# HGRN heads of a fused decoder step: the next head's projections placed between the parts of this head

## The chip, the cores and the metric

One core of a Trainium2 chip runs the whole program. The metric is the device time of one execution in microseconds (us).

## The reference, cut to what matters

The model is a two-layer decoder step for 512 prompt positions and 8 sample sequences of one position each. Layer 0 mixes tokens with two groups of heads side by side: 8 HGRN2 heads and Mamba heads. The change is in the HGRN2 heads alone. For one head, with a forget gate f, a query q, a value v and an output gate g, all four projected from the same normalised input h (1024 wide, 128 columns per head and projection):

```python
q_a, f_a, i_a, g_a, ... = split(h @ w_in_ab)
log_f = log(lb + (1 - lb) * sigmoid(f));  k = (1 - lb) * sigmoid(-f);  q = silu(q)
S_t = diag(f_t) S_{t-1} + k_t v_t^T       # state, 128 x 128 a head
o_t = S_t^T q_t                           # prompt in chunks, samples one step each
out = rmsnorm(o) * hg_norm * silu(g)
```

The prompt is computed in chunks: inside a chunk the attention of queries over keys with the decay between them, across chunks through the state. The samples take one step each from a stored state.

## The kernel before

All data lie feature-major: 128 features on the partitions, 520 tokens (512 prompt, 8 sample) along the free axis, held in PSUM as two banks of 260 columns. Weights arrive from HBM in a ring of two slots (`weight_ring`), one load of 1 MB holding a head's query and forget weights, the next its value and gate weights. A projection is done in three passes, for nearly full float32 precision: weights rounded to fp32r times rounded inputs ("hi"), bf16 weights times the inputs' remainder, and the weights' remainder in bf16 times bf16 inputs ("rest"). Each pass is 8 tiles x 2 halves, 16 matmuls of 260 columns. ScalarE makes the hi and bf16 copies of the weights (`hgrn_cut`, L1616 and L1617) and VectorE the remainder (`hgrn_cut`, L2381); two buffers of weight parts take turns, so a cut waits for the projection before last.

Each engine has one instruction stream in a fixed order written out by hand, with semaphores between them. For each of the 8 heads (`head(h, more)` on each engine, a hardware loop for seven and the last one apart), the order on TensorE is: VALUE projection (banks 6, 7); GATE projection (banks 4, 5), with the five transposes of the values ahead of its rest pass (L1127, they wait for ScalarE's copy of the values, L1833); the key-query products of "level 0" and level 64 (L1152); four transposes of the decayed keys (L1133); the products of the other six levels (L1152), each of which waits until VectorE has taken the one before last out of the two PSUM banks; the four state updates of the chunks (L1159); the values of the samples spread to all partitions (L1163, banks 6, 7); the FORGET projection of the next head (banks 2, 3); the prompt's outputs (L1175, L1177); the samples' outputs, eight matmuls of one column (L1181, 16 instructions in the trace); the QUERY projection of the next head (banks 0, 1) with the sum of squares (L867, `sums`) after its hi pass.

ScalarE has, per head: the cut of the GATE weights; SiLU of the query (L1823); the exponentials of the cumulated decay, of the keys' decay and of seven levels (L1826 to L1831); the copy of the values (L1833); the token-major values (L1835 to L1837); SiLU of the gate (L1839); the cuts of the next FORGET and QUERY; the copy of the transposed keys (L1847); the samples' products of key and value (`sample_products`, L1808); the next head's two sigmoids (`forget_gates`, L1801 and L1802) and the cut of VALUE; the squares of the outputs (L1855, L1856); the logarithm of the next forget gate (`forget_log`, L1814); the inverse RMS (`inv_rms`, L1572 and L1574).

VectorE has, per head: remainder of GATE (L2381); fourteen subtractions for the level decays (L2441, L2442) and fourteen multiplications by queries and keys (L2453, L2454); remainders of the next FORGET and QUERY; the three bf16 parts of the sample values (L2462 to L2467); the eight levels taken out of PSUM (L2482, L2475, L2485), L2488; the update of the eight sample states (L2494, eight operations; `s_new`); the states of the chunks (L2499, L2502; `h_s`); `forget` of the next head (L2422, L2423, remainder of VALUE, and L2426, the scan that cumulates the logarithm); the normalised output (L2509, L2510, L2513; `h_done`).

GpSimd loads and stores the states by DMA, SyncE loads the weights.

## Time and profile before

| | us |
|---|---|
| median of 3 runs (lowest, highest) | 3025.14 (3020.88, 3027.26) |
| the profiled execution, its time | 3025.36 |
| its span in the profile | 3023.8 |
| TensorE matmuls busy | 2807.6 (93%) |
| VectorE busy | 1406.4 (47%) |
| ScalarE busy | 1355.1 (45%) |
| mean granted TensorE clock | 0.969 of 2.4 GHz |

The HGRN heads lie from 499 us to 839 us of the span. How to read the rows below: a time ahead of a line is the start of the first instruction of a merged run, the next number is how long the run took, `xN` how many instructions it holds, and the bracket at the end is the idle time of that engine before it and what ended it. A run that begins before the one ahead of it has ended is pipelined. PEclk is the granted TensorE clock: 1.00 is 2.4 GHz, 0.50 is 1.2 GHz.

### The profile page before, as it was taken

The page shows a single profiled execution, that of the slowest core. Times are in us where ns is not written, and L with a number is a line of the kernel's source. Part 1 is how long each engine was busy: PE and PEld are TensorE (multiplying, and loading weights), DVE is VectorE, ACT ScalarE, POOL GpSimd, SP SyncE. Part 2 cuts the span into 40 slices and gives each one's busy share as a digit, 9 for nine tenths or more (in the row PEclk, how much of TensorE's full clock was granted, in tenths as well). Part 3 has the DMA queues.
Part 4 walks back from the last instruction along what each step waited for, and adds up shares of the span by engine and source line. Part 5 has one row for each costly group of instructions (what it writes and reads, how often), then busy time and mean ns, then how long its engine had stood idle before and what let it go on. Part 6 is the DMA issues. An engine that isn't in the chain of part 4 may idle for free.

```text
span 3023.8 us, 60783 instructions
## 1 busy us (share of the span) xinstructions
PE 2807.6 (93%) x24504; PEld 2354.1 (78%) x24504; DVE 1406.4 (47%) x2893; ACT 1355.1 (45%) x2099; POOL 45.1 (1%) x78
## 2 busy tenths in 40 slices
PE   6999997887888989999999999999989989999997
PEld 3899885777667868799888899888856557789996
DVE  2444327666657763634425444333433434544433
ACT  3444337666643444634345434344423334544443
POOL 0000000000000000000000000000000000000000
PEclk8999998989999989999999999999999999999998
DMA  6223442121212224222343123432365435322221
GB/s 241 84 97 123 161 148 86 71 85 64 78 68 89 88 94 184 89 83 95 138 177 117 70 97 123 166 143 79 128 187 161 148 112 191 123 74 94 102 96 67
DMA packets 58281, 349.35 MB, mean 116 GB/s; under 512 B 7537, under 2 KB 7874, under 8 KB 28578
## 3 DMA queue, kind: packets, MB, share of 16 engines
q1 hardware_dynamic: 52274, 322.85, 30.0%
q0 software_dynamic: 5872, 24.59, 2.3%
q8 instruction: 98, 1.61, 0.2%
q14 instruction: 37, 0.30, 0.0%
HBM read 334.96 MB, written 12.45 MB: 115 GB/s over the span
## 4 chain that ended last, share of the span: by engine, by line
PE 76%; DVE 8%; ACT 8%; issue 3%; DVEq 2%; DMA 2%; ACTq 0%; PEldq 0%; SPq 0%; POOL 0%; PEld 0%
PE PS L940 54%; PE PS L918 2%; PE PS L954 2%; PE PS L867 2%; PE PS L1436 1%; PE PS L978 1%; PE PS L1418 1%; PE PS L1421 1%; PE PS L874 1%; PE PS L1397 1%; ACT hgrn_w_hi L1616 1%; DMA weight_ring<-in_mla_pairs 1%; PE PS L899 1%; ACT sub_out L1831 1%; PE PS L962 1%
## 5 line engine op out<-in xcount | busy, mean ns | idle before, releaser
L2167 DVE TENSOR_TENSOR w_rest<-weight_ring,w_hi 128x1024 bf16<-128x1024 f32 (+1 forms) x268 | 320.8, 1197 | 857.4 <-ACT w_hi L1616 857.2
L1616 ACT ACTIVATE w_hi<-weight_ring 128x1024 fp32r<-128x1024 f32 (+1 forms) x284 | 294.8, 1038 | 889.1 <-PE PS L940 886.0
L940 PE MATMUL PS<-hid_hi,w_hi 128*128 128x260 f32 x2432 | 326.9, 286 | 0.0
L940 PEld LDWEIGHTS PS<-hid_hi,w_hi 128*128 128x128 f32 x2432 | 299.2, 188 | 2.3
L940 PE MATMUL PS<-hid_rest,w_bf 128*128 128x260 bf16 x2432 | 298.4, 274 | 0.0
L940 PE MATMUL PS<-hid_bf,w_rest 128*128 128x260 bf16 x2432 | 296.7, 274 | 0.0
L1617 ACT ACTIVATE w_bf<-weight_ring 128x1024 bf16<-128x1024 f32 (+1 forms) x284 | 289.7, 1020 | 0.0
L940 PEld LDWEIGHTS PS<-hid_bf,w_rest 128*128 128x128 bf16 x2432 | 235.6, 97 | 36.5
L940 PEld LDWEIGHTS PS<-hid_rest,w_bf 128*128 128x128 bf16 x2432 | 223.9, 97 | 38.6
L940 PE MATMUL PS<-gu_hi,w_hi 128*128 128x260 f32 x1232 | 168.7, 288 | 0.0
L940 PEld LDWEIGHTS PS<-gu_hi,w_hi 128*128 128x128 f32 x1232 | 152.8, 188 | 14.1 <-issue 11.2
L940 PE MATMUL PS<-gu_rest,w_bf 128*128 128x260 bf16 x1232 | 152.3, 274 | 0.0
L940 PE MATMUL PS<-gu_bf,w_rest 128*128 128x260 bf16 x1232 | 151.3, 273 | 0.0
L940 PEld LDWEIGHTS PS<-gu_bf,w_rest 128*128 128x128 bf16 x1232 | 119.1, 97 | 18.6
L940 PE MATMUL PS<-hgrn_in_rest,hgrn_w_bf 128*128 128x260 bf16 x1056 | 133.0, 276 | 0.0
L940 PE MATMUL PS<-hgrn_in_bf,hgrn_w_rest 128*128 128x260 bf16 x1056 | 130.7, 274 | 0.0
L940 PE MATMUL PS<-mixer_in_hi,hgrn_w_hi 128*128 128x260 f32 x864 | 122.7, 297 | 6.3 <-ACT hgrn_w_hi L1616 5.1
L940 PEld LDWEIGHTS PS<-gu_rest,w_bf 128*128 128x128 bf16 x1232 | 112.8, 97 | 19.7
L940 PEld LDWEIGHTS PS<-mixer_in_hi,hgrn_w_hi 128*128 128x128 f32 x864 | 112.3, 198 | 9.7 <-ACT hgrn_w_hi L1616 5.4
L940 PEld LDWEIGHTS PS<-hgrn_in_bf,hgrn_w_rest 128*128 128x128 bf16 x1056 | 102.3, 97 | 16.2
L940 PEld LDWEIGHTS PS<-hgrn_in_rest,hgrn_w_bf 128*128 128x128 bf16 x1056 | 97.5, 98 | 18.7
L874 PE MATMUL PS<-consts 128*128 128x512 bf16 x337 | 86.6, 414 | 2.9 <-DVEq L558 2.9
(487 smaller groups left out, 4471.8 us busy)
## 6 DMA issues: line engine op xcount, KB each, us to landing
weight_ring<-in_ffn_gu SPq DMA_DIRECT2D x88, 1024.0 KB, 4.8
ada_chunks<-in_ada_w SPq DMA_DIRECT2D x40, 1536.0 KB, 6.6
weight_ring<-in_ffn_wd SPq DMA_DIRECT2D x32, 1408.0 KB, 6.0
weight_ring<-in_w_hgrn SPq DMA_DIRECT2D x16, 1024.0 KB, 4.8
weight_ring<-in_ada_w SPq DMA_DIRECT2D x8, 1536.0 KB, 7.2
weight_ring<-in_w_ssm SPq DMA_DIRECT2D x8, 1536.0 KB, 6.9
weight_ring<-in_mla_pairs SPq DMA_DIRECT2D x8, 1536.0 KB, 6.5
weight_ring<-in_w_out_ab SPq DMA_DIRECT2D x8, 1024.0 KB, 7.9
```

What stands on the lines that cost most here:

```text
L867: last = pe.matmul(PS[0:rows, bank + hf, 0:HT], weights[k], moving[k][:, hf * HT:(hf + 1) * HT], start=(k == 0), stop=(k == n - 1))
L874: pe.matmul(PS[:, bank, :], STEADY[:, 0:P], STEADY[:, 0:4 * P], start=True, stop=True)
L899: last = pe.matmul(PS[:, bank, 0:HT], w[:, k * P:(k + 1) * P], x[:, k, side(hf)], start=start and w is w_hi, stop=stop and w is w_rest)
L918: last = pe.matmul(PS[:, bank, 0:HT], w[:, k * P:(k + 1) * P], x[:, first + k, side(hf)], start=start and w is w_hi and k == 0, stop=stop ...
L940: last = pe.matmul(PS[:, bank + hf, 0:HT], w[:, k * P:(k + 1) * P], x[:, first + k, hf * HT:(hf + 1) * HT], start=start and w is w_hi and ...
L954: last = pe.matmul(PS[q * QR_:(q + 1) * QR_, 4, 0:3 * P], CS[:, k, :], weights[:, k * 3 * P:(k + 1) * 3 * P], start=(k < 4), stop=(k >= 4))
L962: last = pe.matmul(PS[:, 5, c * NSEQ:(c + 1) * NSEQ], MS[:, c * P:(c + 1) * P], const("fold")[:, 0:NSEQ], start=True, stop=True)
L978: last = pe.matmul(PS[:, 7, 0:HT], ONES, Y[:, c, side(hf)], start=(c == 0), stop=(c == DC - 1))
L1397: last = pe.matmul(PS[:, 4, :], WF[:, first:first + P], CKV[:, k, 0:NP_], start=(k == 0), stop=(k == RC - 1))
L1616: act.activation(hi, src, ACT.Copy).then_inc(w_hi_ready, 1)
L1617: act.activation(bf, src, ACT.Copy).then_inc(w_bf_ready, 1)
L2167: tt(WL_[:, buf, 0:n], W[:, slot, j * DC * P:j * DC * P + n], WH[:, buf, 0:n].bitcast(F32), ALU.subtract).then_inc(w_rest_ready, 1)
```

## The change

On TensorE a head now runs: all eight levels without a break; the transposes of the keys; FORGET of the next head (banks 2, 3); the state updates; the spread of the sample values; QUERY of the next head; the outputs of prompt and samples; VALUE of the next head (now banks 2, 3), with the sum of squares behind its hi pass; GATE of the next head, with the next head's value transposes ahead of its rest pass (now in banks 2, 3). The first head's VALUE and GATE stand ahead of the loop. In the last head 12 and 24 filler matmuls stand where FORGET and QUERY would be, instead of 30.

On ScalarE the cut of the next FORGET moves ahead of the token-major value copies, the next sigmoids and the cut of VALUE ahead of the samples' products, the logarithm of the next forget gate behind those and ahead of the squares, and the cut of GATE from the next head's start to behind the squares. On VectorE the eight levels come directly after the multiplications, ahead of the remainders of FORGET and QUERY and of the sample values; the chunk states and `forget` of the next head come ahead of the update of the sample states, for which the eight sample columns of the gate and the key are copied first (`FS`, `KS`).

```diff
--- before.py
+++ after.py
@@ -285,6 +285,7 @@
         V3 = yar.take(P // 2, rows=NB3).bitcast(BF16)
         VR = yar.take(P, rows=NB)
         VM = yar.take(P // 2, rows=NB).bitcast(BF16)
+        FS, KS = yar.take(NB), yar.take(NB)
         S0 = ar.take(NB, P)
         VK = ar.take(NB, P)
         assert ar.at <= HGRN_END
@@ -1115,27 +1116,26 @@
                 tail()
 
             def hgrn():
-                def project(h, c, bank, between=None, late=False):
-                    product_by_pass(hgrn_group(h, c), bank, c % 2, DC, 0, GHH, GHB, GHL, True, True,
+                def project(h, c, bank, between=None, late=False, ahead=0):
+                    product_by_pass(hgrn_group(h, c) + 4 * ahead, bank, c % 2, DC, 0, GHH, GHB, GHL, True, True,
                                     (GWH, GWB, GWL), between, late).then_inc(part_done, 1)
 
+                def values_and_gate(h, ahead, sums=None):
+
+                    def values_by_token():
+                        pe.wait_ge(h_vf, h + ahead + 1)
+                        for c in range(NCH):
+                            pe.transpose(PS[:, 2, c * P:(c + 1) * P], VF[:, c * CH:(c + 1) * CH], IDENT)
+                        pe.transpose(PS[0:NB, 3, 0:P], VF[:, NP_:T], IDENT).then_inc(h_vt, 1)
+
+                    pe.wait_ge(h_exp, h * 3 + (3 * ahead + 1))
+                    project(h, VALUE, 2, sums, False, ahead)
+                    if ahead:
+                        pe.wait_ge(h_r, h + 1)
+                    project(h, GATE, 4, values_by_token, True, ahead)
+
                 def head(h, more):
 
-                    def values_by_token():
-                        pe.wait_ge(h_vf, h + 1)
-                        for c in range(NCH):
-                            pe.transpose(PS[:, 6, c * P:(c + 1) * P], VF[:, c * CH:(c + 1) * CH], IDENT)
-                        pe.transpose(PS[0:NB, 7, 0:P], VF[:, NP_:T], IDENT).then_inc(h_vt, 1)
-
-                    def keys_by_token():
-                        pe.wait_ge(h_exp, h * 3 + 3)
-                        for c in range(NCH):
-                            last = pe.transpose(PS[:, 4, c * P:(c + 1) * P], KD[:, c * CH:(c + 1) * CH], IDENT)
-                        last.then_inc(h_kt, 1)
-
-                    pe.wait_ge(h_done, h + 1)
-                    project(h, VALUE, 6)
-                    project(h, GATE, 4, values_by_token, True)
                     pe.wait_ge(h_kd, h + 1)
                     for n in range(1 + len(LEVELS)):
 
@@ -1152,21 +1152,30 @@
                                 last = pe.matmul(PS[at:at + m, n % 2, col:col + m], lhs[:, keys:keys + m],
                                                  rhs[:, queries:queries + m], start=True, stop=True)
                         last.then_inc(h_p, 1)
-                        if n == 1:
-                            keys_by_token()
+                    pe.wait_ge(h_exp, h * 3 + 3)
+                    for c in range(NCH):
+                        last = pe.transpose(PS[:, 4, c * P:(c + 1) * P], KD[:, c * CH:(c + 1) * CH], IDENT)
+                    last.then_inc(h_kt, 1)
+                    pe.wait_ge(h_v, h + 1)
+                    if more:
+                        project(h, FORGET, 2, None, False, 1)
+                    else:
+                        keep_busy(2, 12)
                     pe.wait_ge(h_kdt, h + 1)
                     for c in range(NCH):
                         last = pe.matmul(PS[:, 5, c * P:(c + 1) * P], KDT[:, c, :], VV[:, c, :], start=True, stop=True)
                     last.then_inc(h_u, 1)
                     pe.wait_ge(h_vs, h + 1)
+                    pe.wait_ge(h_done, h + 1)
                     for b in range(NB):
                         last = pe.matmul(PS[:, 6 + b // 4, (b % 4) * P:(b % 4 + 1) * P], SEL[:, b * P:(b + 1) * P], V3,
                                          start=True, stop=True)
                     last.then_inc(h_vb, 1)
                     if more:
-                        project(h + 1, FORGET, 2)
+                        pe.wait_ge(h_ptk, h * 8 + 10)
+                        project(h, QUERY, 0, None, False, 1)
                     else:
-                        keep_busy(2, 30)
+                        keep_busy(2, 24)
                     pe.wait_ge(h_vk, h + 1)
                     pe.wait_ge(h_att, h + 1)
                     pe.wait_ge(h_s, h + 1)
@@ -1187,7 +1196,7 @@
                         product(4, [ONES], [SQO]).then_inc(h_ss, 1)
 
                     if more:
-                        project(h + 1, QUERY, 0, sums)
+                        values_and_gate(h, 1, sums)
                     else:
                         sums()
 
@@ -1216,6 +1225,7 @@
 
                 first_projections()
                 pe.wait_ge(vec_in, 64)
+                values_and_gate(0, 0)
                 with pe.Fori(0, HG - 1) as h:
                     head(h, True)
                 head(HG - 1, False)
@@ -1806,7 +1816,7 @@
                     act.wait_ge(h_vb, h + 1)
                     for b in range(NB):
                         last = act.activation(VK[:, b, :], PS[:, 6 + b // 4, (b % 4) * P:(b % 4 + 1) * P],
-                                              ACT.Identity, scale=KK[:, NP_ + b:NP_ + b + 1])
+                                              ACT.Identity, scale=KS[:, b:b + 1])
                     last.then_inc(h_vk, 1)
 
                 def forget_log(h, ahead=0):
@@ -1816,9 +1826,9 @@
                 forget_gates(0)
                 cut(0, VALUE)
                 forget_log(0)
+                cut(0, GATE)
 
                 def head(h, more):
-                    cut(h, GATE)
                     projected(h, QUERY)
                     act.activation(two(QS), pair(0), ACT.Silu).then_inc(h_exp, 1)
                     both_tables()
@@ -1830,34 +1840,38 @@
                         act.wait_ge(h_d, h * 9 + (3 + n))
                         act.activation(DL[:, n, :], DL[:, n, :], ACT.Exp).then_inc(h_ex, 1)
                     projected(h, VALUE)
-                    act.activation(two(VF), pair(6), ACT.Copy).then_inc(h_vf, 1)
+                    act.activation(two(VF), pair(2), ACT.Copy).then_inc(h_vf, 1)
+                    if more:
+                        cut(h, FORGET, 1)
+                    else:
+                        ssm_cut(0, 0)
                     act.wait_ge(h_vt, h + 1)
-                    act.activation(VS, PS[0:NB, 7, 0:P], ACT.Copy)
-                    act.activation(V3[0:NB], PS[0:NB, 7, 0:P], ACT.Copy)
-                    act.activation(VV.rearrange("p a b -> p (a b)"), PS[:, 6, :], ACT.Copy).then_inc(h_v, 1)
+                    act.activation(VS, PS[0:NB, 3, 0:P], ACT.Copy)
+                    act.activation(V3[0:NB], PS[0:NB, 3, 0:P], ACT.Copy)
+                    act.activation(VV.rearrange("p a b -> p (a b)"), PS[:, 2, :], ACT.Copy).then_inc(h_v, 1)
                     projected(h, GATE)
+                    act.wait_ge(h_done, h + 1)
                     act.activation(two(GS), pair(4), ACT.Silu).then_inc(h_exp, 1)
                     if more:
-                        cut(h, FORGET, 1)
+                        act.preload_act_table_set("sigmoid_and_others")
                         cut(h, QUERY, 1)
                     else:
-                        ssm_cut(0, 0)
                         ssm_cut(0, 1)
                     act.wait_ge(h_kt, h + 1)
                     act.activation(KDT.rearrange("p a b -> p (a b)"), PS[:, 4, :], ACT.Copy).then_inc(h_kdt, 1)
                     if more:
-                        act.preload_act_table_set("sigmoid_and_others")
-                    sample_products(h)
-                    if more:
                         forget_gates(h, 1)
                         cut(h, VALUE, 1)
+                    else:
+                        both_tables()
+                    sample_products(h)
+                    if more:
+                        forget_log(h, 1)
                     act.wait_ge(h_o, h * 2 + 2)
                     act.activation(SQO[:, 0:NP_], PS[:, 6, :], ACT.Square)
                     act.activation(SQO[:, NP_:T], PS[:, 7, 0:NB], ACT.Square).then_inc(h_sq, 1)
                     if more:
-                        forget_log(h, 1)
-                    else:
-                        both_tables()
+                        cut(h, GATE, 1)
                     act.wait_ge(h_ss, h + 1)
                     inv_rms(h_r, P, bank=4)
 
@@ -2452,21 +2466,6 @@
                         k = KK[:, 0:NP_].rearrange("p (a c b) -> p a c b", c=2, b=m)
                         tt(d[:, :, 1, :], d[:, :, 1, :], q[:, :, 1, :], ALU.mult)
                         tt(d[:, :, 0, :], d[:, :, 0, :], k[:, :, 0, :], ALU.mult).then_inc(h_qk, 1)
-                    if more:
-                        cut(h, FORGET, 1)
-                        cut(h, QUERY, 1)
-                    else:
-                        ssm_cut(0, 0)
-                        ssm_cut(0, 1)
-                    dve.wait_ge(h_v, h + 1)
-                    tt(VR, VS, V3[0:NB], ALU.subtract)
-                    dve.drain()
-                    dve.tensor_copy(VM, VR)
-                    dve.drain()
-                    tt(V3[64:64 + NB], VR, VM, ALU.subtract)
-                    dve.tensor_copy(V3[32:32 + NB], VM)
-                    dve.drain().then_inc(h_vs, 1)
-
                     for n in range(1 + len(LEVELS)):
                         dve.wait_ge(h_p, h * 8 + (n + 1))
                         if n in (1, 2):
@@ -2487,12 +2486,24 @@
                     for at in range(0, CH, QR_):
                         dve.tensor_copy(AT[at:at + QR_, :, at:at + QR_], AB[at:at + QR_])
                     dve.drain().then_inc(h_att, 1)
-
-                    dve.wait_ge(s_loaded, h * 16 + 16)
-                    dve.wait_ge(h_vk, h + 1)
-                    for b in range(NB):
-                        last = stt(S0[:, b, :], S0[:, b, :], FG[:, NP_ + b:NP_ + b + 1], VK[:, b, :], ALU.mult, ALU.add)
-                    last.then_inc(s_new, 1)
+                    if more:
+                        cut(h, FORGET, 1)
+                    else:
+                        ssm_cut(0, 0)
+                    dve.wait_ge(h_v, h + 1)
+                    tt(VR, VS, V3[0:NB], ALU.subtract)
+                    dve.drain()
+                    dve.tensor_copy(VM, VR)
+                    dve.drain()
+                    tt(V3[64:64 + NB], VR, VM, ALU.subtract)
+                    dve.tensor_copy(V3[32:32 + NB], VM)
+                    dve.tensor_copy(KS, KK[:, NP_:T])
+                    dve.drain().then_inc(h_vs, 1)
+                    if more:
+                        cut(h, QUERY, 1)
+                    else:
+                        ssm_cut(0, 1)
+
 
                     dve.wait_ge(h_u, h + 1)
                     dve.wait_ge(s_stored, h + 1)
@@ -2502,8 +2513,17 @@
                         stt(ST[:, c, :], ST[:, c - 1, :], EB[:, (c + 1) * CH - 1:(c + 1) * CH],
                             PS[:, 5, c * P:(c + 1) * P], ALU.mult, ALU.add)
                     dve.drain().then_inc(h_s, 1)
-                    if more:
+                    dve.wait_ge(s_loaded, h * 16 + 16)
+                    if more:
+                        dve.tensor_copy(FS, FG[:, NP_:T])
                         forget(h, 1)
+                    else:
+                        dve.tensor_copy(FS, FG[:, NP_:T])
+                        dve.drain()
+                    dve.wait_ge(h_vk, h + 1)
+                    for b in range(NB):
+                        last = stt(S0[:, b, :], S0[:, b, :], FS[:, b:b + 1], VK[:, b, :], ALU.mult, ALU.add)
+                    last.then_inc(s_new, 1)
 
                     dve.wait_ge(h_r, h + 1)
                     tt(R[:, 0:NP_], R[:, 0:NP_], PS[:, 6, :], ALU.mult)
```

## Rows read from the trace of the kernel before

**Rows 1.** Line 2513 in the whole stage: duration min/median/max, first to last start.
```profile
L2513 DVE SCALAR_TENSOR_TENSOR arena<-inv_rms,arena x8: 760/760/761, 543.4 to 838.6; 128x520 f32 x7, 128x520 f32<-128x520 f32 x1
```

**Rows 2.** The same line from 790 us on (last two heads).
```profile
L2513 DVE SCALAR_TENSOR_TENSOR arena<-inv_rms,arena x2: 760/760/761, 797.9 to 838.6; 128x520 f32 x1, 128x520 f32<-128x520 f32 x1
```

**Rows 3.** Timeline, TensorE, one head: start, us, engine, line, x count [idle before].
```profile
714.34 2.17 PE L940 MATMUL PS<-mixer_in_hi,hgrn_w_hi 128*128 128x260 f32 x16
...
719.86 2.17 PE L940 MATMUL PS<-mixer_in_hi,hgrn_w_hi 128*128 128x260 f32 x16
...
725.11 0.66 PE L1127 MATMUL PS<-consts,arena 128*128 128x128 f32 x4 [1.27 <-ACT arena L1833]
...
734.88 3.60 PE L1152 MATMUL PS<-sub_out 128*32 128x32 f32 x176 [5.44 <-DVE weight_parts L2482]
738.41 1.16 PE L1159 MATMUL PS<-arena 128*128 128x128 f32 x8
...
739.82 2.16 PE L940 MATMUL PS<-mixer_in_hi,hgrn_w_hi 128*128 128x260 f32 x16
...
746.17 0.68 PE L1175 MATMUL PS<-arena 128*128 128x128 f32 x4 [0.59 <-DVEq L2504]
...
747.80 1.84 PE L1181 MATMUL PS<-arena 128*128 128x1 f32 x16
749.51 2.16 PE L940 MATMUL PS<-mixer_in_hi,hgrn_w_hi 128*128 128x260 f32 x16
751.51 1.04 PE L867 MATMUL PS<-arena,consts 128*128 128x260 f32 x4
...
755.96 2.17 PE L940 MATMUL PS<-mixer_in_hi,hgrn_w_hi 128*128 128x260 f32 x16
```

**Rows 4.** Timeline, VectorE, the same head.
```profile
715.64 1.23 DVE L2381 TENSOR_TENSOR hgrn_w_rest<-weight_ring,hgrn_w_hi 128x1024 bf16<-128x1024 f32 x1 [0.70 <-ACT hgrn_w_hi L1616]
...
717.68 0.42 DVE L2441 TENSOR_TENSOR sub_out<-arena 128x256 f32<-128x256 f32 x1
...
727.95 0.43 DVE L2454 TENSOR_TENSOR sub_out<-sub_out,arena 128x256 f32<-128x256 f32 x1
...
734.53 0.29 DVE L2482 TENSOR_TENSOR weight_parts<-PS,consts 128x128 f32<-128x128 f32 x1 [0.19 <-issue]
...
742.34 2.19 DVE L2494 SCALAR_TENSOR_TENSOR arena<-arena 128x128 f32<-128x128 f32 x8 [2.23 <-ACT arena L1808]
...
751.13 1.23 DVE L2426 TENSOR_TENSOR_SCAN arena<-mixer_consts,arena 128x512 f32<-128x512 f32 x1 [0.80 <-ACT arena L1814]
...
756.40 0.15 DVE L2432 COPY arena<-arena 128x1 f32 x1 [0.59 <-issue]
```

**Rows 5.** Timeline, ScalarE, the same head.
```profile
724.48 0.58 ACT L1833 ACTIVATE arena<-PS 128x520 f32<-128x520 f32 x1
...
740.05 2.18 ACT L1808 ACTIVATE arena<-PS,arena 128x128 f32<-128x128 f32 x8 [5.75 <-PE PS L1163]
...
748.02 1.06 ACT L1616 ACTIVATE hgrn_w_hi<-weight_ring 128x1024 fp32r<-128x1024 f32 x1
...
750.47 0.63 ACT L1814 ACTIVATE arena<-arena 128x512 f32<-128x512 f32 x1
```

**Rows 6.** Timeline, TensorE, the filler matmuls of the last head.
```profile
824.49 6.64 PE L874 MATMUL PS<-consts 128*128 128x512 bf16 x30
```

**Rows 7.** Timeline, TensorE, a Mamba group: one-column matmuls, then a projection.
```profile
917.95 3.73 PE L1306 MATMUL PS<-arena,sub_out 128*128 128x1 f32 x32
921.54 3.06 PE L940 MATMUL PS<-mixer_in_hi,hgrn_w_hi 128*128 128x260 f32 x16
```

**Rows 8.** Windows: us, busy (x) per engine, TensorE granted clock, DMA share, GB/s.
```profile
734.88:738.14 3.26, 3.09 (x156) 2.70 (x160) 1.89 (x6) 0.00 (x0) 0.00 (x0) 0.50 0.67 281
744.50:749.51 5.01, 4.42 (x40) 4.05 (x39) 2.79 (x9) 3.87 (x5) 1.20 (x2) 1.00 0.24 97
921.54:924.40 2.86, 2.86 (x18) 2.76 (x17) 2.60 (x5) 0.00 (x0) 0.00 (x0) 0.66 0.03 6
```

More of the change, by code:

```diff
@@ L1848, in head @@
                     if more:
-                        act.preload_act_table_set("sigmoid_and_others")
+                        forget_gates(h, 1)
+                        cut(h, VALUE, 1)
+                    else:
+                        both_tables()
                     sample_products(h)
                     if more:
-                        forget_gates(h, 1)
-                        cut(h, VALUE, 1)
+                        forget_log(h, 1)
                     act.wait_ge(h_o, h * 2 + 2)
```

## The prediction

> **What bounds the kernel now.** The page comes first: TensorE is busy for 93% of the span, VectorE and ScalarE for under half. That share is an average over stages; the change touches only the HGRN heads, so what counts is where TensorE stands still there. The last VectorE operation of a head (line 2513) starts at 543.4 us in head 0 and at 838.6 us in head 7 [rows 1], at 797.9 us in head 6 [rows 2]: six periods of (797.9 - 543.4) / 6 = 42.4 us, and a last head of 40.7 us. Next the timeline of TensorE through one head [rows 3]. VALUE starts at 714.34 and again at 755.96: 41.6 us in this head, so the average head loses 0.8 us to something that this one does not. TensorE stands 1.27 us ahead of the value transposes (ScalarE's value copy comes after seven exponentials), 5.44 us ahead of the last six levels (VectorE, which does two weight remainders and the sample values before it looks at level 0), and 0.59 us ahead of the outputs. 7.3 of 41.6 us are idle: a head is a ring in which VectorE and ScalarE work while TensorE waits.
>
> The clock is the other half. In the level products that follow the 5.44 us of idleness the granted clock is 0.50, the lower level of 1.2 GHz; where only 0.59 us were idle it is 1.00, 2.4 GHz, with the one-column products included [rows 8]. Those 0.8 us of the average head are what is left of the low level when dense work resumes. In the Mamba stage one-column products fill TensorE for 3.7 us and the projection behind them takes 3.06 us for its hi pass [rows 7], at a clock of 0.66 [rows 8], against 2.17 us in [rows 3]: TensorE's record is busy there, its clock falls as if it were idle.
>
> **The change, walked through one head.** The count of matmuls of a full head stays, and so does the work on the other two engines but for two copies of eight columns, so the sum is a new ring. Let 0 be the start of VALUE.
>
> 1. The hi pass takes 2.00 us, then the sum of squares starts (749.51 to 751.51, [rows 3]). From the start of that sum to the first copy of the next head on VectorE (line 2432) are 4.89 us (751.51 to 756.40, [rows 3, 4]), with ScalarE's inverse root and line 2513 inside. Time 6.9. The cut of GATE on ScalarE now fits between the squares and the inverse root, 0.96 to 2.95 us, and doesn't delay it. This takes the wait for ScalarE's cut at the start of a head (0.70 us, [rows 4]) away.
> 2. Remainder of GATE at 7.05, first subtraction 2.04 us on (715.64 to 717.68 in [rows 4]), 9.1; the last multiplication ends 10.7 us later (717.68 to 727.95 and 0.43), 19.8. Nothing lies between it and the levels now: 5.4 us of remainders and waits before line 2482 are gone from here. The first level is taken out at 19.9.
> 3. From there the six levels need 3.88 us of TensorE and VectorE taking turns (734.53 to 738.41, [rows 3, 4]), 23.8; four key transposes 0.5 us (as the value transposes, 725.11 and 0.66 with its tail), 24.3.
> 4. FORGET starts at 24.3 and takes 5.5 us (714.34 to 719.86, [rows 3]), 29.8. Its remainder is cut behind the levels on VectorE, from about 25.8 to 27.0, and wanted at 28.1: hidden, with 1 us to spare. States and spread 1.41 us (738.41 to 739.82), 31.2. QUERY 5.5 us, 36.75. Prompt outputs 1.63 us (746.17 to 747.80), 38.4.
> 5. The ring through ScalarE: from the start of FORGET to the start of the cut of VALUE, sigmoids and table load included, are 8.20 us (739.82 to 748.02, [rows 3, 5]), 32.5. The cut is two passes of 1.06 us, overlapping a little, 34.45. The samples' products 2.18 us [rows 5], 36.6. The logarithm to the start of the scan 0.66 us (750.47 to 751.13, [rows 4, 5]), 37.3. The scan 1.23 us, 38.5. Now the eight updates of the sample states, 2.19 us [rows 4], which before the change ran ahead of all this: 40.8. The samples' outputs wait for them.
> 6. So TensorE stands from 38.4 to 40.9, 2.5 us where before there were 0.59 us; the samples' outputs take 1.71 us (747.80 to 749.51), and the next VALUE starts at 42.6. Behind that wait are queued VALUE and GATE of the next head, and ScalarE's squares.
>
> The first half of the head has a longer wait too: VALUE with the sum ends at 6.45 (749.51 to 755.96), GATE's first two passes at 10.4 (719.86 to 725.11 less 1.27), while the copy of the values comes one exponential and 0.58 us [rows 5] behind the last subtraction, at 15.0. TensorE stands 4.6 us there instead of 1.27. Added up: 4.6 + 1.5 (level 2 waits for VectorE) + 2.5 idle against 7.3, so the ring is 1.0 us longer than the undisturbed one of 41.6, and 0.2 us longer than the average.
>
> **The clock.** No row shows a wait of 2.5 us followed by 1.7 us of one-column products. Its bounds are 0 (the 0.59 us case, clock 1.00) and 2.9 us (VALUE's hi pass and the sum, both twice as long). The nearest row is the Mamba one, 3.7 us of such products, which makes the hi pass 0.9 us longer; the sum behind it suffers a part of its 0.9 us. I take 1.3 us, all of it on the ring, since step 1 starts with the sum. The 4.6 us wait is nearly the 5.44 us one, so I expect 0.50 there also; but value transposes and the rest pass of GATE at half speed end at 19.4 to 19.7 instead of 17.4, just when VectorE gets to the levels: 0.3 us (bounds 0 and 2.3). The average 0.8 us of before goes away with the 5.44 us wait and is already in the 42.4.
>
> The Trainium skill, "TensorE: Matmul & The Clock Gate", section "A second HAM failure mode: psum-queue depth-cycling", has a kernel whose many tiny idle stretches between matmul groups made the clock go back and forth, the price being paid at each return. Here short idleness of 0.59 us left 1.00 standing; by that rule the new ring, with three waits instead of one long one, would pay at each, which is the third rival below.
>
> **The ends.** Head 0 is the same up to the end of its multiplications; from there on it runs as the ring does, about 1.5 us later at line 2513 (1.0 for the ring, 1.3 for the clock, less 0.8 that it lost). The last head: transposes end at 24.3, 12 fillers of 0.22 us [rows 6] to 26.9, states and spread (which waits for VectorE's sample values, 28.3) to 28.9, 24 fillers to 34.2; products and updates end at 33.8 beneath them; outputs 1.63, then from the samples' outputs to line 2513 about 6.1 us, as in step 1: 41.9. Line 2513 of head 6 is at 5.5, so 36.4, with 0.3 of clock 36.7: 4.0 us less than 40.7, as the last head has no projection to do.
>
> **Sum.** Period 42.6 + 1.3 + 0.3 = 44.2, six times 1.8 over 42.4: +10.8. Head 0 +1.5, last head -4.0. Together +8.3 us on the profiled execution's own 3025.4 us (span 3023.8), which is 0.2 us from the median shown, 3025.1. Forecast 3033.5 us, slower.
>
> **Rivals.** A measurement of this kernel can tell about 0.2% from no change, 6 us.
> - The clock holds: 42.6 us a head, head 0 +0.2, last -4.3: -3 us, 3022 us. For it: only 2.5 us are truly idle. Against it: [rows 7, 8]. 0.20.
> - Half of it: the low level falls in only every other head, or mostly on passes with slack behind the sum. Period 43.4, 3028 us. 0.13.
> - The low level lasts over VALUE and the sum and again over GATE and the first levels in each head: 46 us a head, about +21, 3046 us. For it: the clock after idleness stays at 0.50 through sparse work [rows 8]. 0.13.
> - The other side: the wait at the samples' outputs doesn't bind, because the sigmoids, the cut and the products on ScalarE come 2.5 us earlier than I have them. It decides from the moment that line 2494 ends before the prompt outputs do, at 38.4. The period is then 40.1 us: 6 x -2.3 - 4 = -18, 3007 us. For it: the change takes 5.44 us of idleness away. Against it: step 5 is a chain of durations read off rows, and needs 16.5 us behind FORGET where TensorE has 14.1 us of work. 0.12.
> - The forecast itself: 0.42, of its own range 3029 to 3039.
>
> Range 3019 to 3045 us: the lower end takes in the case of a held clock, the upper nearly the long low level. Faster by over 0.2%: 0.13. Within: 0.33 (held clock, half of it, none of the rest). Slower: 0.54.
>
> **What would show it.** Line 2513 44 us apart in heads 1 to 6 and about 37 in the last; TensorE idle about 4.6 us ahead of line 1127's successor, about 1.5 us inside the levels, and about 2.5 us ahead of the samples' outputs, ended by VectorE's update of the sample states; VALUE's hi pass behind them 2.9 us or so at a granted clock of about 0.6; FORGET at 1.00. If the samples' outputs follow the prompt's without a gap, step 5 is wrong and the kernel is faster; if the gap is there and VALUE's hi pass takes 2.2 us, the clock term is.

## The result, and the profile after

The changed kernel takes 3038.95 us (median of 5 runs, 3034.68 to 3044.85) against 3025.71 us (5 runs, 3020.88 to 3027.26): a ratio of 1.0046, 95% interval 1.0032 to 1.0060. It is slower, by about half a per cent. Its profiled execution is its fastest run, 3034.68 us with a span of 3033.1 us; the profiles differ by 9.3 us, the medians by 13.2.

The last operation of a head on VectorE is line 2533 now. Its row over the whole stage, and from 800 us on:

```profile
L2533 DVE SCALAR_TENSOR_TENSOR arena<-inv_rms,arena x8: 759/761/762, 549.2 to 850.6; 128x520 f32 x7, 128x520 f32<-128x520 f32 x1
```

```profile
L2533 DVE SCALAR_TENSOR_TENSOR arena<-inv_rms,arena x2: 761/761/761, 814.5 to 850.6; 128x520 f32 x1, 128x520 f32<-128x520 f32 x1
```

Six periods of (814.5 - 549.2) / 6 = 44.2 us where [rows 1, 2] gave 42.4, and a last head of 36.1 us where they gave 40.7. The stage ends 12.0 us later. Of that, 10.7 us come from the six periods, 5.8 from head 0, and -4.6 from the last head. Of the 5.8 us, 2.3 lie ahead of the first VALUE (501.6 us instead of 499.3), where both kernels run the same instructions. The span grew by 2.7 us less than the stage, and the change touches nothing behind it either. Both amounts are within what single executions differ by: over the thirteen profiled executions of this document the first VALUE starts at 497.1 to 503.3 us, and the part behind the stage takes 2181 to 2193 us.

One head on TensorE, the rows that answer to [rows 3] (start, us, line, count, idle before):

```profile
723.26 1.04 PE L868 MATMUL PS<-arena,consts 128*128 128x260 f32 x4
...
736.31 0.76 PE L1128 MATMUL PS<-consts,arena 128*128 128x128 f32 x4 [4.71 <-ACT arena L1843]
...
737.07 3.45 PE L941 MATMUL PS<-hgrn_in_bf,hgrn_w_rest 128*128 128x260 bf16 x16
...
740.84 3.82 PE L1152 MATMUL PS<-sub_out 128*64 128x64 f32 x184
744.58 0.66 PE L1157 MATMUL PS<-consts,arena 128*128 128x128 f32 x4
745.00 2.16 PE L941 MATMUL PS<-mixer_in_hi,hgrn_w_hi 128*128 128x260 f32 x16
...
757.49 0.61 PE L1184 MATMUL PS<-arena 128*128 128x128 f32 x4
...
761.40 1.95 PE L1190 MATMUL PS<-arena 128*128 128x1 f32 x16 [2.20 <-DVE arena L2525]
763.21 3.13 PE L941 MATMUL PS<-mixer_in_hi,hgrn_w_hi 128*128 128x260 f32 x16
766.15 1.69 PE L868 MATMUL PS<-arena,consts 128*128 128x260 f32 x4
767.68 1.95 PE L941 MATMUL PS<-hgrn_in_rest,hgrn_w_bf 128*128 128x260 bf16 x16
```

The 5.44 us wait ahead of the levels is gone: 184 of the level matmuls follow each other from 740.84, and in these six heads TensorE waits nowhere in the levels. In its place stand 4.71 us ahead of the value transposes and 2.20 us ahead of the samples' outputs, 759.2 to 761.4, ended by the update of the sample states. Behind that wait VALUE's hi pass takes 3.13 us and the sum 1.69 us. In the period before this one (head 4) the same wait weighs more:

```profile
716.34 3.57 PE L1190 MATMUL PS<-arena 128*128 128x1 f32 x16 [2.19 <-DVE arena L2525]
719.77 3.65 PE L941 MATMUL PS<-mixer_in_hi,hgrn_w_hi 128*128 128x260 f32 x16
```

From 716.34 to 719.77 the granted clock is 0.50, so the products take twice their time too, and this period is 45.9 us long. The six periods are 43.6, 44.1, 44.1, 45.9, 43.5 and 44.1 us.

Through six heads, all that TensorE waited for (us in total, times, longest):

```profile
PE PS L1128 <- ACT arena L1843: 28.0, 6, 4.7
PE PS L1190 <- DVE arena L2525: 13.2, 6, 2.2
```

VectorE and ScalarE in the same head, the rows that answer to [rows 4, 5]:

```profile
728.15 0.15 DVE L2446 COPY arena<-arena 128x1 f32 x1 [0.59 <-issue]
728.28 1.23 DVE L2395 TENSOR_TENSOR hgrn_w_rest<-weight_ring,hgrn_w_hi 128x1024 bf16<-128x1024 f32 x1
...
740.98 0.29 DVE L2481 TENSOR_TENSOR weight_parts<-PS,consts 128x128 f32<-128x128 f32 x1
...
757.82 1.23 DVE L2440 TENSOR_TENSOR_SCAN arena<-mixer_consts,arena 128x512 f32<-128x512 f32 x1 [1.84 <-ACT arena L1824]
759.16 2.19 DVE L2525 SCALAR_TENSOR_TENSOR arena<-arena,sub_out 128x128 f32<-128x128 f32 x8
```

```profile
753.20 1.06 ACT L1626 ACTIVATE hgrn_w_hi<-weight_ring 128x1024 fp32r<-128x1024 f32 x1
...
755.11 2.16 ACT L1818 ACTIVATE arena<-PS,sub_out 128x128 f32<-128x128 f32 x8
757.11 0.68 ACT L1824 ACTIVATE arena<-arena 128x512 f32<-128x512 f32 x1
```

ScalarE goes from the cut of VALUE (753.20) to the products (755.11) and the logarithm (757.11) without a pause, VectorE from the scan (757.82) to the update (759.16), and TensorE starts 2.24 us behind that. This is the ring of the prediction's step 5, to within 0.2 us. Four stretches of the same head (columns as in [rows 8]; the clock is the third number from the end):

```profile
761.40:763.21 1.81, 1.80 (x16) 1.81 (x17) 0.00 (x0) 0.00 (x0) 0.53 (x1) 1.00 0.07 27
763.21:766.15 2.94, 2.94 (x19) 2.94 (x19) 0.00 (x0) 2.55 (x4) 0.00 (x0) 0.64 0.40 162
736.31:740.45 4.14, 4.14 (x22) 2.87 (x22) 4.14 (x13) 3.91 (x6) 0.00 (x0) 0.59 0.00 0
745.00:750.59 5.59, 5.59 (x52) 5.08 (x51) 4.66 (x12) 0.60 (x1) 0.00 (x0) 1.00 0.00 0
```

In this head the one-column products run at 1.00; behind them, in VALUE's hi pass, the clock is 0.64; in the value transposes and GATE's rest pass behind the long wait 0.59; in FORGET 1.00 again.

### The profile page after: what moved, and what is told of

It is laid out like the page before. It is cut to its first block, busy times and chain, and to the rows that moved or that the text cites. A ratio compares the mean times of both kernels' runs of the same rounds, so it can differ in the third digit from the quotient of the medians.

```text
span 3033.1 us, 60848 instructions
## 1 busy us (share of the span) xinstructions
PE 2827.0 (93%) x24510; PEld 2365.3 (78%) x24510; DVE 1407.9 (46%) x2909; ACT 1361.4 (45%) x2099; POOL 44.4 (1%) x78
## 4 chain that ended last, share of the span: by engine, by line
PE 78%; DVE 9%; ACT 6%; issue 3%; DVEq 2%; DMA 1%; ACTq 0%; PEldq 0%; SPq 0%; POOL 0%; PEld 0%
PE PS L941 56%; PE PS L919 3%; PE PS L955 2%; PE PS L868 2%; PE PS L979 1%; PE PS L1446 1%; PE PS L1428 1%; PE PS L1431 1%; PE PS L1342 1%; PE PS L963 1%; PE PS L1407 1%; PE PS L875 1%; PE PS L900 1%; DVE arena L2765 1%; PE PS L1438 1%
## 5 line engine op out<-in xcount | busy, mean ns | idle before, releaser
L941 PEld LDWEIGHTS PS<-gu_hi,w_hi 128*128 128x128 f32 x1232 | 152.8, 188 | 14.1 <-issue 11.2
L941 PE MATMUL PS<-hgrn_in_bf,hgrn_w_rest 128*128 128x260 bf16 x1056 | 142.4, 289 | 0.0
L941 PEld LDWEIGHTS PS<-mixer_in_hi,hgrn_w_hi 128*128 128x128 f32 x864 | 117.5, 206 | 10.1 <-issue 8.1
```

Of the source, the lines that this page charges most:

```text
L941: last = pe.matmul(PS[:, bank + hf, 0:HT], w[:, k * P:(k + 1) * P], x[:, first + k, hf * HT:(hf + 1) * HT], start=start and w is w_hi and ...
```

## The experiments

Each was run in five rounds beside the kernel before, the last one in three. The period is that of the profiled execution, from line 2513 or its counterpart of head 0 to head 6, divided by six. Time moves with the chip and the hour (the kernel before had medians of 3022 to 3028 us), so the ratios (to the kernel before in the same rounds) are to be compared. The last column is TensorE's wait in one head ahead of the value transposes and ahead of the samples' outputs.

| run | us | ratio (95%) | period | wait, values / samples |
|---|---|---|---|---|
| before | 3025.7 | 1 | 42.4 | 1.3 / 0 |
| changed | 3039.0 | 1.0046 (1.0032 to 1.0060) | 44.2 | 4.7 / 2.2 |
| 1 sample work first | 3007.7 | 0.9936 (0.9924 to 0.9949) | 40.0 | 4.7 / 0 |
| 2 samples' wait filled, 10 wide | 3033.4 | 1.0020 (1.0010 to 1.0031) | 43.7 | 4.7 / filled |
| 3 values' wait filled | 3046.4 | 1.0057 (1.0041 to 1.0073) | 44.9 | filled / 2.2 |
| 4 before, levels' wait filled | 3023.5 | 0.9991 (0.9981 to 1.0002) | 41.2 | 1.3 / 0 |
| 5 update ahead of scan | 3009.7 | 0.9957 (0.9940 to 0.9973) | 41.2 | 4.7 / 0.3 |
| 6 as 2, 20 float32r fillers | 3020.3 | 0.9987 (0.9977 to 0.9997) | 42.3 | 4.7 / filled |
| 7 as 1, values' wait filled | 3004.1 | 0.9935 (0.9920 to 0.9949) | 40.2 | filled / 0 |
| 8 before, levels first | 3017.9 | 0.9982 (0.9972 to 0.9991) | 41.6 | 1.3 / 0 |
| 9 as 7, float32r fillers | 3010.8 | 0.9939 (0.9925 to 0.9954) | 40.2 | filled / 0 |
| 10 as 2, bf16 inputs | 3034.1 | 1.0019 (1.0010 to 1.0027) | 43.8 | 4.7 / filled |
| 11 as 10, 20 narrow | 3022.4 | 1.0000 (0.9990 to 1.0009) | 42.2 | 4.7 / filled |

**1. The sample work first.**

```diff
 ScalarE, behind the copy of the transposed keys:
+                    sample_products(h)
                     if more:
                         forget_gates(h, 1)
                         cut(h, VALUE, 1)
-                    sample_products(h)
-                    if more:
                         forget_log(h, 1)
 (shortened) VectorE: the eight updates of S0 (s_new) ahead of forget(h, 1), not behind it
```

> The changed kernel with one thing put back: ScalarE's products for the samples and VectorE's update of the eight sample states run again ahead of the next head's sigmoids, cut of VALUE, logarithm and scan. Theory (the ring of a head closes through that chain, and TensorE's 2.2 us wait ahead of the samples' outputs, with the fall of the clock behind it, is the price): no wait ahead of the samples' outputs, the hi pass of VALUE back at 2.0 us, 40.4 us from head to head instead of 44.2, about 27 us less than the changed kernel: 3012 us, faster than before. Rival A (the order on TensorE is at fault, the 4.7 us wait ahead of the value transposes above all; the other wait has slack behind it): the idle time moves to another place, 43 to 44 us a head, 3032 to 3039 us.

40.0 us a head and 3007.7 us, where the theory had 40.4 and 3012. TensorE in one head of it:

```profile
714.09 1.12 PE L1128 MATMUL PS<-consts,arena 128*128 128x128 f32 x4 [4.71 <-ACT arena L1843]
...
715.21 3.67 PE L941 MATMUL PS<-hgrn_in_bf,hgrn_w_rest 128*128 128x260 bf16 x16
...
736.38 0.61 PE L1184 MATMUL PS<-arena 128*128 128x128 f32 x4
...
737.94 1.84 PE L1190 MATMUL PS<-arena 128*128 128x1 f32 x16
739.65 2.16 PE L941 MATMUL PS<-mixer_in_hi,hgrn_w_hi 128*128 128x260 f32 x16
741.64 1.04 PE L868 MATMUL PS<-arena,consts 128*128 128x260 f32 x4
```

From 736.38 the prompt outputs, the samples' outputs, VALUE's hi pass and the sum follow each other without a gap, in 2.0 us for the hi pass. The 4.7 us wait is still there, with GATE's rest pass at 3.67 us behind it. Rival A falls: the new order on TensorE is not at fault; put together with the old order of the sample work it is 0.6% faster than the kernel before.

**5. The update of the states ahead of the scan**, the smallest edit with that effect, on VectorE alone:

```diff
                     cut(h, VALUE, ahead)
+                    update()          # shortened: wait for h_vk, the eight updates of S0, s_new
                     dve.wait_ge(h_lf, h + (ahead + 1))
```

> The changed kernel with VectorE's order alone altered: the update of the sample states directly ahead of the scan, ScalarE's order untouched. Theory: the state update ends at 36.6 + 2.2 = 38.8 us behind the start of VALUE instead of 40.8, TensorE waits 0.5 us ahead of the samples' outputs instead of 2.2, and such a short wait leaves the clock at 1.00: 40.5 to 41 us from head to head, about 3.5 us less than the changed kernel's 44.2, 24 us in all: 3015 us. Rival (price of the wait without its clock, or of the clock alone): 42.5 us a head, 3027 us.

TensorE's wait ahead of the samples' outputs, summed over six heads:

```profile
PE PS L1190 <- DVE arena L2522: 2.0, 6, 0.3
```

A wait of 0.3 us, periods of 40.1 to 42.4, on average 41.2, and 3009.7 us. Four of six heads are 40.1 to 40.8 us long; in the two of 42.4 us the clock fell at the samples' outputs all the same. TensorE waits 0.3 us in both kinds of head, so the length of the wait does not tell them apart. Next to the one-column products the clock fell at the samples' outputs in two of the seven heads with this wait and in none of seven without one (run 1).

**2, 6, 10, 11. The samples' wait filled**, the wait itself kept:

```diff
                     last.then_inc(h_o, 1)
+                    if more:
+                        pe.wait_ge(h_exp, h * 3 + 4)
+                        keep_busy(2, 10)             # 2: 512 columns, table of zeros and ones
                     pe.wait_ge(s_new, h + 1)
 6:  20 x matmul(PS[:, 2, 0:HT], GWH[:, 0, tile k % 8], GHH[:, k % 8, 0:HT])   # float32r
 10: 10 x matmul(PS[:, 2, :], GWB[:, 0, tile 0], GHB[:, k % 8, 0:512])          # bf16
 11: 20 x matmul(PS[:, 2, 0:HT], GWB[:, 0, tile k % 8], GHB[:, k % 8, 0:HT])   # bf16
```

> The changed kernel with 10 filler matmuls of 512 columns (about 2.2 us) in TensorE's wait ahead of the samples' outputs, in heads 0 to 6; the wait and the work stay. Theory: the one-column products and the wait together count as idleness; with the wait filled the granted clock stays at 1.00 through VALUE's hi pass and the sum, 1.3 us less a head: 42.9 us from head to head, about 9 us less than the changed kernel, 3030 us. Rival B (the lower clock falls on work with slack, or the one-column products alone bring it down): no difference, 3039 us, VALUE's hi pass still about 3 us.

> The changed kernel with its wait ahead of the samples' outputs filled by 20 matmuls of 260 columns on the weights and inputs of VALUE's hi pass (2.2 us), instead of the 10 fillers of the earlier run, which work on a table of zeros and ones and left the clock falling in five heads of seven. Theory 1 (fillers on zeros and ones count for less): the clock holds, VALUE's hi pass 2.0 us, 42.9 us a head, 3029 us. Theory 2 (the one-column products alone bring the clock down wherever they fall): as with the other fillers, 43.7 us a head, 3033 us.

> The changed kernel with its wait ahead of the samples' outputs filled by 10 bf16 matmuls of 512 columns, as many, as wide and of the same type as the fillers that let the clock fall in five heads of seven, but on VALUE's bf16 weights and the bf16 inputs instead of the table of zeros and ones. Theory (the data decide): clock held, as with the float32 fillers on such data, 42.3 us from head to head, 3020 us. Rival (the type or the width decides): 43.7 us, 3033 us.

> The changed kernel with its wait ahead of the samples' outputs filled by 20 bf16 matmuls of 260 columns with eight weight tiles in turn on VALUE's bf16 weights: as the 20 float32r fillers that held the clock (42.3 us a head) but for the type. If the type decides: the clock falls as with the ten wide bf16 fillers, 43.5 to 44 us a head, 3033 us. If the width or the change of weights decides: clock held, 42.3 us, 3021 us.

(The diffs of runs 6, 10 and 11 are shortened to their filler; each also waits first for the weights that it reads.)

Filler, one-column products and VALUE's hi pass in one head of runs 2, 6, 10 and 11, in this order:

```profile
579.47 2.11 PE L875 MATMUL PS<-consts 128*128 128x512 bf16 x9
581.61 1.95 PE L1193 MATMUL PS<-arena 128*128 128x1 f32 x16
583.42 3.13 PE L941 MATMUL PS<-mixer_in_hi,hgrn_w_hi 128*128 128x260 f32 x16
```

```profile
573.78 2.63 PE L1192 MATMUL PS<-mixer_in_hi,hgrn_w_hi 128*128 128x260 f32 x20
576.25 1.92 PE L1196 MATMUL PS<-arena 128*128 128x1 f32 x16
578.03 2.16 PE L941 MATMUL PS<-mixer_in_hi,hgrn_w_hi 128*128 128x260 f32 x16
```

```profile
579.54 2.32 PE L1192 MATMUL PS<-hgrn_in_bf,hgrn_w_bf 128*128 128x512 bf16 x10
581.90 1.95 PE L1195 MATMUL PS<-arena 128*128 128x1 f32 x16
583.70 2.62 PE L941 MATMUL PS<-mixer_in_hi,hgrn_w_hi 128*128 128x260 f32 x16
```

```profile
576.73 2.38 PE L1192 MATMUL PS<-hgrn_in_bf,hgrn_w_bf 128*128 128x260 bf16 x20
579.10 1.95 PE L1196 MATMUL PS<-arena 128*128 128x1 f32 x16
580.90 2.16 PE L941 MATMUL PS<-mixer_in_hi,hgrn_w_hi 128*128 128x260 f32 x16
```

With ten wide fillers TensorE has no wait left ahead of the products, and in these heads the hi pass is still 2.62 and 3.13 us long; the period is 43.8 and 43.7 us. With twenty narrow ones of about the same duration the clock held in all seven heads, the hi pass takes 2.16 us, and the period is 42.3 and 42.2 us. The ten fillers let the clock fall on other data too (run 10 against run 2), and the twenty hold it in either type (run 11 against run 6): my theory that zeros and ones were at fault fell. The stretches of runs 10 and 11 are equally long (2.36 and 2.37 us) and of nearly as many columns (5120 and 5200). What differs is the width, the number, and the weight tiles, one for all ten against eight in turn; the weight loads are busy for 0.88 us of the stretch in run 10 and for 1.86 us in run 11. Which of these it is was not taken apart.

The gain of run 6 on the changed kernel is the price of the clock behind the samples' wait: 44.2 - 42.3 = 1.9 us a head. The wait itself is the rest of what run 1 takes away: 42.3 - 40.0 = 2.3 us. Together they are the 4.2 us between the changed kernel and run 1. No run has a wait of 2.2 us without the one-column products behind it, so how much of the fall the wait alone would bring is not shown.

**3, 7, 9. The values' wait filled.**

```diff
                     def values_by_token():
+                        if ahead:
+                            pe.wait_ge(h_exp, h * 3 + 5)
+                            keep_busy(0, 20)         # 3, and 7 on top of 1
                         pe.wait_ge(h_vf, h + ahead + 1)
 9: on top of 1, 38 x matmul(PS[:, 0, 0:HT], GWH[:, 1, tile k % 8], GHH[:, k % 8, 0:HT])
```

> The changed kernel with 20 filler matmuls (4.4 us) in TensorE's wait ahead of the value transposes (4.7 us idle), in heads 1 to 7. Theory: the granted clock is 1.00 in the rest pass of GATE, which then takes 1.8 us instead of 3.5, but VectorE gets to the levels no earlier: 0.3 us a head, 2 us in all, 3037 us, not to be told from the changed kernel. Rival A (this wait and its clock are the loss): 1.7 us a head and more, 3027 us or less.

The waits of run 3 in TensorE's rows:

```profile
PE PS L1193 <- DVE arena L2528: 15.4, 7, 2.2
PE PS L1155 <- DVE weight_parts L2484: 8.4, 6, 1.4
PE PS L1131 <- ACT arena L1846: 2.0, 5, 0.5
```

The long wait is down to 0.4 us, the levels now wait 1.4 us for VectorE in each head, and nothing is gained: the levels start when VectorE says so. That the run is slower than the changed kernel was not expected. In five heads of seven the low clock at the samples' outputs lasted 6.8 us instead of 3.4 (two of seven in the changed kernel), so that it covers the products too. Two rows of one such head:

```profile
629.01 2.99 PE L1193 MATMUL PS<-arena 128*128 128x1 f32 x16 [2.19 <-DVE arena L2528]
631.86 3.81 PE L941 MATMUL PS<-mixer_in_hi,hgrn_w_hi 128*128 128x260 f32 x16
```

In three heads it also fell in the levels, as in run 9 below: around 702 us the key transposes take 1.12 us and FORGET's hi pass 2.94. So the clock that was held in GATE was lost again behind it. Why a held clock in GATE makes the next fall longer is open.

> The run with the sample products and states first (40.0 us a head, 3007.7 us), with 20 filler matmuls in the 4.7 us wait ahead of the value transposes in heads 1 to 7. In that run heads in which GATE's rest pass took 3.6 us at the lower clock were 40.3 to 40.6 us long, those with a shorter low stretch 39.3. Theory: the clock holds through GATE's rest pass and the first levels, every head 39.3 us, 5 us less: 3003 us. Rival (the waits of VectorE set the levels' start whatever the clock does; fillers spill over): 40.0 us or more, 3008 us.

> The run with the sample products and states first, with its 4.7 us wait ahead of the value transposes filled by 38 matmuls of 260 columns on GATE's weights and the inputs (4.3 us) instead of fillers on zeros and ones, which let the clock fall in five heads of seven. Theory: the granted clock is 1.00 in every head, 39.3 us from head to head instead of 40.1, about 5 us less than with the other fillers: 2999 us, the fastest version. Rival (the clock falls there through the sparse level products, not through the wait): 40.1 us, 3004 us.

Both came out where run 1 is: 40.2 us a head and ratios of 0.9935 and 0.9939 against 0.9936. 39.3 us was reached in one head of six. Run 9, behind a filled wait:

```profile
709.28 4.77 PE L1129 MATMUL PS<-mixer_in_hi,hgrn_w_hi 128*128 128x260 f32 x38
...
719.20 3.55 PE L1157 MATMUL PS<-sub_out 128*32 128x32 f32 x176 [1.40 <-DVE weight_parts L2485]
722.68 1.07 PE L1162 MATMUL PS<-consts,arena 128*128 128x128 f32 x4
```

The clock holds through GATE's rest pass and falls in the sparse level products instead, after 719.20, so that the key transposes take 1.07 us and not 0.66: the rival was right. Neither filler brought anything in this wait.

**4. The kernel before with its wait filled.**

```diff
                         if n == 1:
                             keys_by_token()
+                            keep_busy(2, 22)
```

> The kernel before with 22 filler matmuls (4.8 us) in its 5.4 us wait ahead of the six levels. Theory: what the average head (42.4 us) lost against the undisturbed one (41.6 us) was the clock: every head 41.6 us, 0.8 us times 7 or 8 less, about 3019 us. Rival: the spread came from elsewhere (DMA of states and weights), no difference, 3025 us.

The fillers and the levels behind them:

```profile
727.74 4.70 PE L874 MATMUL PS<-consts 128*128 128x512 bf16 x21
733.12 3.20 PE L1152 MATMUL PS<-sub_out 128*32 128x32 f32 x176 [0.69 <-DVE weight_parts L2483]
```

Each of the six periods is 41.2 us; without the fillers they were 41.6 to 43.1. The spread of the kernel before was the clock, and 1.2 us a head are its price, not the 0.8 that the least disturbed head suggested. The whole kernel's gain, 0.9991 (0.9981 to 1.0002), is not clear of none, where the theory had 3019 us. Six periods that are 1.2 us shorter make 7 us; the medians differ by 3.5, and where the rest went is not shown.

**8. One part of the change alone**: in the kernel before, VectorE's block with the remainders of FORGET and QUERY and the sample values moved behind the levels.

> The kernel before with one part of the change alone: on VectorE the eight levels ahead of the remainders of FORGET and QUERY and of the sample values. Theory: TensorE's 5.4 us wait moves from ahead of the levels to ahead of the spread of the sample values, which VectorE has ready 1.2 us earlier (30.3 instead of 31.5 us behind the start of QUERY), but the wait of about 4 us now stands right ahead of FORGET, so the lower clock falls on a whole projection: 41 to 42 us a head instead of 42.4, 3018 to 3027 us. Rival (this order is the gain of the change and needs nothing else): no wait left there, under 40 us a head, 3010 us or less.

TensorE ahead of FORGET in one head:

```profile
734.66 1.03 PE L1163 MATMUL PS<-sub_out,mixer_consts 72*128 72x128 bf16 x8 [4.01 <-DVEq L2489]
735.45 3.81 PE L940 MATMUL PS<-mixer_in_hi,hgrn_w_hi 128*128 128x260 f32 x16
```

As expected, TensorE stands 4.0 us ahead of the spread of the sample values, and FORGET's hi pass behind it takes 3.81 us in this head. The period is 41.6 us, 0.8 less than before, the kernel faster by 0.18% (0.9982, 0.9972 to 0.9991). This part of the change is a small gain.

## Why the prediction was right

It said 3033.5 us, slower; the profiled execution took 3034.7 and the median is 3039.0, inside the range. The mechanism was right: TensorE's new wait ahead of the samples' outputs, ended by the update of the sample states, with the fall of the clock behind it. That the numbers agree so closely is in part luck, as the terms below show. Measured from step to step, the head without the fall at the samples' outputs is 41.95 us long (2.00, 4.89, 0.13, 12.70, 3.60, 0.42 and 18.21), where the steps gave 42.6.

Steps 1 and 2 held: from the sum to line 2446 are 4.89 us (723.26 to 728.15), from the remainder of GATE to the first level 12.70 us (728.28 to 740.98; 12.85 forecast). Beside the steps, the prediction's count of idle time has a slip: 4.6 + 1.5 + 2.5 is 8.6 us, 1.3 and not 1.0 more than 7.3. The sum does not use it.

One sign did not come: the 1.5 us wait inside the levels. It was worked out at full clock. At the low clock the value transposes and GATE's rest pass last until VectorE is ready, as the prediction's own clock paragraph says, and no wait is left there. With the clock held in GATE it is there, 1.4 us (run 3).

Step 3 was 0.3 us too long: 3.60 us from the first level to the key transposes, not 3.88. The transposes and FORGET's start follow in 0.42.

Steps 4 and 5: from FORGET to the cut of VALUE 8.20 us (745.00 to 753.20), as forecast; products at 10.1, logarithm at 12.1, scan at 12.8, update at 14.2, samples' outputs at 16.4, next VALUE at 18.2 (763.21) where 18.3 was forecast. Run 1 shows that this chain is what the new ring costs (4.2 us a head), run 5 that its last link, the scan ahead of the update, carries most of it (3.0 us).

Step 6: the wait is 2.20 us, 2.5 forecast: the prompt outputs ended 14.2 us behind FORGET's start instead of 14.1, the samples' outputs began at 16.4 instead of 16.6.

The clock term at the samples' outputs was mis-sized: 1.3 us forecast, 1.9 us measured by run 6. In the head shown the hi pass and the sum are 1.6 us longer (763.21 to 767.68, 4.47 us against 2.88 at full clock); in the five heads like it they are 1.4 to 1.6 us longer. In head 4 the low level covers the products too: 7.80 us from their start to the end of the sum (716.34 to 724.14) against 4.69 at full clock (1.81 and 2.88), so 3.1 us, more than the prediction's upper bound of 2.9, which left the products out. The mean of the six is 1.8, close to run 6's 1.9. The ring without this term, 42.3 us, is 0.6 us shorter than my 42.9. The two errors cancel by luck: 44.2 forecast, 44.2 measured.

The clock term at GATE (0.3 us) has about the right size. Two periods have a low level of 3.4 us there: they are 43.5 and 43.6 us long, and in the head shown VectorE takes the first level directly behind its multiplications, as it would at full clock. Three others have a low level of 6.8 us there, and are 44.1 us long. In run 6 three periods of the first kind are 41.8 to 41.9 us long and three of the second 42.4 to 43.1. It can't be had back by filling the wait: with the wait filled, the clock falls a little later, in the levels (run 9).

The average loss to the clock in the kernel before was taken as 0.8 us and is 1.2 (run 4).

The last head: 36.1 us, 36.7 forecast. Head 0: +5.8 us instead of +1.5. Of the 4.3 us missing, 2.3 came ahead of the first VALUE; most of the rest is the clock, which in this execution stayed low for 6.8 us around head 0's samples' outputs. So the stage came out 3.7 us longer than forecast, and 2.7 us of it went again behind the stage. That the forecast met the profiled execution's time to 1.2 us is luck of this kind. The medians lie 13.2 us apart and not 9.3, since the changed kernel's profiled run was its fastest: its runs spread over 10 us, those of before over 6. Of the 13.2 us, 8.3 were forecast; only the profiled execution can be taken apart.

The case of many tiny idle stretches that make the clock go back and forth (the Trainium skill, "TensorE: Matmul & The Clock Gate", section "A second HAM failure mode: psum-queue depth-cycling") is borne out in part. The clock of the changed kernel does go back and forth in each head, behind the 4.7 us and the 2.2 us wait; the third wait, in the levels, is not there, and FORGET behind them runs at 1.00. The rival of 46 us a head came true in one period of six (45.9 us, low for 6.8 us at both places); the mean is 44.2.

Of the other rivals, the held clock (42.6 us a head) is what run 6 makes by hand, with 42.3, the low level at GATE included. The rival on the other side (the wait at the samples' outputs doesn't bind, 40.1 us, 3007 us) did not come about, but its arithmetic was right: run 1 takes the wait away and gives 40.0 us and 3007.7 us.

## What to carry to other kernels

When work is spread between the parts of a loop to fill a wait, draw the ring anew on all engines before moving: here a short piece of work that one engine needs at once (the update of the sample states) was queued behind a long chain for the next iteration, and the old wait came back elsewhere. With what another engine waits for in this iteration put first in each queue, the new order gained 0.6% here instead of losing 0.5%. A stretch of one-column matmuls next to a wait is to be priced as part of the wait: here 2.2 us of waiting and 1.8 us of such products brought the clock down in all seven heads, where the kernel before had 1.3 us waits between dense matmuls and kept 1.00 behind each of them.

## What the runs showed of the hardware that was not expected

Fillers are not equal. Ten bf16 matmuls of 512 columns (2.1 and 2.3 us) ahead of 1.8 us of one-column products let the granted clock fall in five and six heads of seven, whether on a table of zeros and ones or on real inputs; twenty matmuls of 260 columns with eight weight tiles in turn (2.4 and 2.5 us), float32r or bf16, held it in every head. These are counts from one profiled execution of each. And holding the clock at one place moved the fall to the next sparse stretch (runs 3 and 9) or went with a longer one (run 3), so a filler has to be judged by the period and not by the stretch it stands in.
